# Two-block transformer kernel: fold order in block 1, last norm's weights on GpSimd, the last expert's slots in column halves

## The reference, cut to what matters

```python
# block 1
h = rmsnorm(x, norm1_g)
p = h @ w_in                                   # 1024 -> 1536: lru_x, lru_gate, four_in
c = centred_depthwise_conv(lru_x, conv_w, conv_b)
y_lru = gelu(lru_gate) * (rglru(c, ..., reverse=False) + rglru(c, ..., reverse=True))
y_four = real(fft2(four_in in 4 groups of 128, axes=(tokens, channels of the group)))
x = x + concat(y_lru, y_four) @ w_out
x = x + expert_choice_moe(rmsnorm(x, norm2_g)) # 16 experts, each takes its 64 best tokens
x = rmsnorm(x, normf_g)
# block 2: band attention, a diagonal state space model, gates
x = x + merged @ w_out_2
return rmsnorm(x, final_gain_2)
```

## Time and profile before

| what | value |
|---|---|
| median of 3 runs | 1468.22 us (1467.8 to 1468.32) |
| the profiled execution: its own time | 1466.85 us |
| the profiled execution: span, first to last instruction | 1465.0 us |
| mean granted TensorE clock | 0.998 of full speed |
| busy share: TensorE, VectorE, ScalarE, GpSimd | 94%, 37%, 23%, 8% |
| the chain that ended last: TensorE, transfers, VectorE, ScalarE | 62%, 30%, 4%, 2% |

### The profile page before, as it was taken

One profiled execution on the slowest core, in us unless ns is written; L12 is line 12 of the kernel. 1 busy time (PEld: TensorE's weight loads), 2 busy tenths in 40 slices (PEclk: granted clock), 3 DMA queues, 4 the chain that ended last, 5 costly groups with the idle time before them and its releaser, 6 DMA issues.

```text
span 1465.0 us, 16663 instructions
## 1 busy us (share of the span) xinstructions
PE 1373.4 (94%) x6713; PEld 737.6 (50%) x6713; DVE 547.6 (37%) x967; ACT 340.0 (23%) x549; POOL 114.5 (8%) x188
## 2 busy tenths in 40 slices
PE   7999999999998898998988988989999999999997
PEld 6778533333333232332322323323378787888876
DVE  7675621121211121121111211113278587756663
ACT  5893110010000010010000100103042465533322
POOL 0000000000000000000000000002022215550000
PEclk9999999999999999999999999999999999999999
DMA  9149899999999999999999999999975132353221
GB/s 324 22 168 390 329 421 405 429 428 429 429 429 429 429 429 429 429 429 429 429 429 429 429 427 429 429 428 428 420 242 132 58 105 83 83 173 133 94 107 58
DMA packets 67875, 467.05 MB, mean 319 GB/s; under 512 B 5744, under 2 KB 30576, under 8 KB 42608
## 3 DMA queue, kind: packets, MB, share of 16 engines
q1 hardware_dynamic: 63008, 454.71, 75.4%
q0 software_dynamic: 4528, 11.18, 3.1%
q10 hardware_dynamic: 288, 0.45, 0.1%
HBM read 458.22 MB, written 7.05 MB: 318 GB/s over the span
## 4 chain that ended last, share of the span: by engine, by line
PE 62%; DMA 30%; DVE 4%; ACT 2%; issue 2%; DVEq 0%; POOL 0%; ACTq 0%
DMA wide<-in_w_up 21%; PE bank L1035 13%; PE bank L975 12%; PE bank L727 8%; PE bank L728 8%; PE bank L729 8%; DMA early<-in_w_up 8%; PE bank L914 4%; PE bank L1005 1%; PE bank L1073 1%; DVE nrm L1749 1%; PE bank L1132 1%; PE bank L1160 1%; PE bank L757 1%; PE bank L762 0%
## 5 line engine op out<-in xcount | busy, mean ns | idle before, releaser
L975 PE MATMUL bank<-wide,xinT 128*64 128x512 f32 x1376 | 307.0, 596 | 41.9 <-DMA wide<-in_w_up 24.4
L975 PEld LDWEIGHTS bank<-wide,xinT 128*64 128x64 f32 x1376 | 96.6, 137 | 248.1 <-issue 170.8
L975 PE MATMUL bank<-early,xinT 128*64 128x512 f32 x656 | 147.0, 595 | 19.4 <-DMA early<-in_w_up 10.7
L1749 DVE SCALAR_TENSOR_TENSOR th<-th,bank 128x512 f32<-128x512 f32 x32 | 20.6, 684 | 385.2 <-ACT th L1458 385.2
L1035 PE MATMUL bank<-wide,actT 128*64 128x512 f32 x656 | 144.9, 594 | 3.6 <-issue 3.5
L727 PE MATMUL bank<-hT_lo,ring_r 128*128 128x512 f32 x352 | 138.6, 394 | 1.4 <-ACT gt L1323 1.1
L729 PE MATMUL bank<-hT_hi,ring_r 128*128 128x512 f32 x352 | 137.1, 390 | 0.0
L728 PE MATMUL bank<-hT_hi,ring_r 128*128 128x512 f32 x352 | 137.0, 389 | 0.0
L1458 ACT ACTIVATE th<-bank 128x512 f32<-128x512 f32 x32 | 17.4, 594 | 475.3 <-PE bank L975 475.3
L1746 DVE TENSOR_TENSOR ring_r<-ring,ring_r 128x2048 fp32r<-128x2048 f32 (+1 forms) x40 | 89.5, 2237 | 59.6 <-ACT ring_r L1291 59.2
L975 PEld LDWEIGHTS bank<-early,xinT 128*64 128x64 f32 x656 | 46.0, 137 | 118.5 <-issue 79.5
(11 more groups left out here) (427 smaller groups left out, 1705.7 us busy)
## 6 DMA issues: line engine op xcount, KB each, us to landing
wide<-in_w_gate SPq DMA_DIRECT2D x43, 2048.0 KB, 37.6
wide<-in_w_up SPq DMA_DIRECT2D x42, 2048.0 KB, 38.0
wide<-in_w_down SPq DMA_DIRECT2D x38, 2048.0 KB, 38.4
early<-in_w_down SPq DMA_DIRECT2D x21, 2048.0 KB, 38.5
early<-in_w_up SPq DMA_DIRECT2D x21, 2048.0 KB, 38.3
early<-in_w_gate SPq DMA_DIRECT2D x20, 2048.0 KB, 39.9
ring<-in_w_in SPq DMA_DIRECT2D x25, 1024.0 KB, 6.2
ring<-in_w_out SPq DMA_DIRECT2D x8, 1024.0 KB, 4.9
```

Of the source, the lines that this page charges most:

```text
L975: last = pe.matmul(bank[1 + 2 * (m % 2) + q // 2][o:o + 64, :], xinT[:, k, :], w[:, i, q * 512:(q + 1) * 512], start=(k == 0), stop=(k == ...
L1749: return dve.scalar_tensor_tensor(out_, a, s, b, op0, op1)
```

## The change

1. `folds()` becomes `even_folds()`, the sums, and `odd_folds()`, the clearing of column 0 and the differences. The scans of the second channel tile come between them. TensorE's `four` jobs are ordered by part first: both products of the sums wait for the first count of `folded`, both of the differences for the second.
2. `slot_hi` and `slot_lo` are made in two passes of 256 columns each; TensorE waits for each half by itself and runs the low products four steps behind the high ones.
3. GpSimd multiplies each merged half row by its weights `gfin` into `hT`, and VectorE's final pass multiplies that by the reciprocal alone. GpSimd's small addition of eps stands in its queue before the odd half row's product.

The diff:

```diff
@@ -353,6 +353,7 @@
         x_sums, gained, gained_sums = sem("x_sums"), sem("gained"), sem("gained_sums")
         x_root = sem("x_root")
         eps_set, deviation = sem("eps_set"), sem("deviation")
+        weighted = sem("weighted")
         gf_half_in, pairs_ready, slot_sums, slot_gained = (
             sem("gf_half_in"), sem("pairs_ready"), sem("slot_sums"), sem("slot_gained"))
         slot_root, slot_high, slot_low, slot_x2_ready, slot_x2_out = (
@@ -365,7 +366,7 @@
             jobs.add(f"xT{k}", k)
 
         order_b1 = [("in", 0), ("in", 1), ("in", 2), ("in", 3), ("lru", 0), ("in", 4), ("in", 5), ("lru", 1), ("in", 6),
-                    ("in", 7), ("lru", 2), ("in", 8)] + [("four", c) for c in range(2)] + [("mid", 0)] + [
+                    ("in", 7), ("lru", 2), ("in", 8)] + [("four", part) for part in range(2)] + [("mid", 0)] + [
             ("in", 9), ("in", 10), ("lru", 3)] + [("mix", g) for g in range(CT)] + [("in", 11)]
         W_LRU, W_DFT = 5, 6
         jobs.turn = 0
@@ -374,8 +375,8 @@
             if what == "in":
                 jobs.add(f"in{n}", unit=in_units[n // 2] if n % 2 else None)
             elif what == "four":
-                for half in range(2):
-                    jobs.add(f"four{n}_{half}")
+                for c in range(2):
+                    jobs.add(f"four{c}_{n}")
             elif what == "lru":
                 for i in range(4):
                     jobs.add(f"lru{n}_{i}", unit=W_LRU if (n, i) == (CT - 1, 3) else None)
@@ -826,15 +827,14 @@
                         split(unit)
                     project(f"in{n}", both(unit, 256), (n % 2) * P, (hT_hi, hT_lo), KT)
                 elif what == "four":
-                    if n == 0:
-                        pe.wait_ge(folded, 2)
-                    for part in range(2):
-                        b = start(f"four{n}_{part}")
-                        rows = (fold, mixT[:, CT:2 * CT, 0:HALF])[part]
+                    pe.wait_ge(folded, n + 1)
+                    rows = (fold, mixT[:, CT:2 * CT, 0:HALF])[n]
+                    for c in range(2):
+                        b = start(f"four{c}_{n}")
                         for g in range(CT):
-                            last = pe.matmul(b[:, g * P:(g + 1) * P], rows[:, g, n * P:(n + 1) * P],
-                                             dft[:, part * P:(part + 1) * P], start=True, stop=True)
-                        finish(f"four{n}_{part}", last)
+                            last = pe.matmul(b[:, g * P:(g + 1) * P], rows[:, g, c * P:(c + 1) * P],
+                                             dft[:, n * P:(n + 1) * P], start=True, stop=True)
+                        finish(f"four{c}_{n}", last)
                 elif what == "mid":
                     b = start("mid")
                     for g in range(CT):
@@ -1047,14 +1047,13 @@
                     other_rows(7)
                     other_rows(3, 4)
                     other_rows(6)
-                    lead = 5
-                    pe.wait_ge(slot_high, 1)
+                    lead = 4
                     for step in range(KT + lead):
-                        if step == lead:
-                            pe.wait_ge(slot_low, 1)
-                        for slots, at in ((slot_hi, step), (slot_lo, step - lead)):
+                        for slots, there, at in ((slot_hi, slot_high, step), (slot_lo, slot_low, step - lead)):
                             if 0 <= at < KT:
                                 k = Y_ORDER[at]
+                                if at % 4 == 0:
+                                    pe.wait_ge(there, at // 4 + 1)
                                 n, c = 64 * (k // 4), (k % 4) * P
                                 last = pe.matmul(bank[k][:, :], slots[n:n + 64, c:c + P], chosenT[n:n + 64, :],
                                                  start=False, stop=(slots is slot_lo))
@@ -1479,7 +1478,9 @@
             act_e.wait_ge(unit_used, last_of[B2_HI[0] // 2] + 1)
             act_e.activation(hi_of(M)[:, 0:UNIT // 2], ring[slot_of(M)][:, 0:UNIT // 2], ACT.Copy)
             act_e.wait_ge(slot_root, 1)
-            act_e.activation(slot_hi, th[:, 0, :], ACT.Copy, scale=stat[:, 50:51]).then_inc(slot_high, 1)
+            for h in range(2):
+                hs = slice(256 * h, 256 * h + 256)
+                act_e.activation(slot_hi[:, hs], th[:, 0, hs], ACT.Copy, scale=stat[:, 50:51]).then_inc(slot_high, 1)
             act_e.activation(hi_of(M)[:, UNIT // 2:UNIT], ring[slot_of(M)][:, UNIT // 2:UNIT], ACT.Copy).then_inc(w_hi, 1)
             scaled_hi("yT", "gb2", Y_ORDER)
             weights_hi(M + 1)
@@ -1727,10 +1728,15 @@
             pool.dma_start(yT, y_dram.rearrange("(c p) t j -> p c (t j)", p=P)).then_inc(y_in, 16)
             full(pool, f"pv{PAIRS - 1}")
             pool.dma_start(gfin, gfin_d.partition_broadcast(P)).then_inc(gfin_in, 16)
-            for t in range(TT):
-                c = stat[:, 48 + t:49 + t]
-                pool.wait_ge(square_sum, 2 * TT + 2 * t + 1)
-                pool.tensor_scalar(c, stat[:, 40 + 2 * t:41 + 2 * t], 1.0, EPS, ALU.mult, ALU.add).then_inc(half_sum, 1)
+            pool.wait_ge(gfin_in, 16)
+            for o in range(2 * TT):
+                t, h = o // 2, slice(o % 2 * 512, o % 2 * 512 + 512)
+                if o % 2:
+                    pool.wait_ge(square_sum, 2 * TT + o)
+                    pool.tensor_scalar(stat[:, 48 + t:49 + t], stat[:, 39 + o:40 + o], 1.0, EPS, ALU.mult,
+                                       ALU.add).then_inc(half_sum, 1)
+                was_read(pool, f"fin{o}")
+                pool.tensor_tensor(hT[:, o, :], added[:, t, h], gfin[:, h], ALU.mult).then_inc(weighted, 1)
 
         @block.vector
         def _(dve):
@@ -1828,13 +1834,17 @@
                     link(dve.tensor_tensor_scan(h, a, b, 0.0, ALU.mult, ALU.add))
                 tt(conv[:, c, :], gt[:, 0, 0, :], gt[:, 1, 0, :], ALU.add).then_inc(gt_free, 1)
 
-            def folds():
+            def even_folds():
                 for g in range(CT):
                     was_read(dve, f"in{CT + g}")
                 f = mixT[:, CT:2 * CT, :]
                 dve.tensor_copy(fold[:, :, 0:1], f[:, :, 0:1])
-                link(tt(fold[:, :, 1:HALF], f[:, :, 1:HALF], f[:, :, S - 1:HALF:-1], ALU.add))
-                dve.memset(f[:, :, 0:1], 0.0).then_inc(folded, 1)
+                tt(fold[:, :, 1:HALF], f[:, :, 1:HALF], f[:, :, S - 1:HALF:-1], ALU.add).then_inc(folded, 1)
+                dve.wait_ge(folded, 1)
+
+            def odd_folds():
+                f = mixT[:, CT:2 * CT, :]
+                link(dve.memset(f[:, :, 0:1], 0.0))
                 tt(f[:, :, 1:HALF], f[:, :, 1:HALF], f[:, :, S - 1:HALF:-1], ALU.subtract).then_inc(folded, 1)
 
             def unfold(g):
@@ -1869,8 +1879,9 @@
             recurrence_scans(0)
             weights_lo(4)
             recurrence_inputs(1)
-            folds()
+            even_folds()
             recurrence_scans(1)
+            odd_folds()
             weights_lo(W_DFT)
             weights_lo(7)
             recurrence_inputs(2)
@@ -2095,9 +2106,11 @@
             last_full(6, 2)
             link(dve.tensor_scalar(stat[:, 48:49], bank[6][:, 0:1], EPS, None, ALU.add))
             stt(stat[:, 49:50], stat[:, 48:49], EPS, bank[6][:, 1:2], ALU.mult, ALU.add).then_inc(bank_read[6], 1)
-            dve.wait_ge(slot_high, 1)
             dve.wait_ge(slot_gained, 1)
-            stt(slot_lo, th[:, 0, :], stat[:, 50:51], slot_hi, ALU.mult, ALU.subtract).then_inc(slot_low, 1)
+            for h in range(2):
+                hs = slice(256 * h, 256 * h + 256)
+                dve.wait_ge(slot_high, h + 1)
+                stt(slot_lo[:, hs], th[:, 0, hs], stat[:, 50:51], slot_hi[:, hs], ALU.mult, ALU.subtract).then_inc(slot_low, 1)
             dve.wait_ge(w_hi, split_units.index(M) + 1)
             halves_of = [tuple(v[:, i * UNIT // 2:(i + 1) * UNIT // 2] for v in (ring_r[slot_of(M)], ring[slot_of(M)], hi_of(M)))
                          for i in range(2)]
@@ -2405,9 +2418,9 @@
                     dve.wait_ge(deviation, TT + t + 1)
                     link(dve.reciprocal(stat[:, 52 + t:53 + t], stat[:, 52 + t:53 + t]))
                 for h in hs:
-                    r = added[:, t, 512 * h:512 * h + 512]
-                    stt(r, r, stat[:, 52 + t:53 + t], gfin[:, 512 * h:512 * h + 512], ALU.mult,
-                        ALU.mult).then_inc(final_ready, 1)
+                    dve.wait_ge(weighted, 2 * t + h + 1)
+                    dve.tensor_scalar(added[:, t, 512 * h:512 * h + 512], hT[:, 2 * t + h, :], stat[:, 52 + t:53 + t], None,
+                                      ALU.mult).then_inc(final_ready, 1)
 
             def merged_row(o):
                 r = added[:, o // 2, o % 2 * 512:o % 2 * 512 + 512]
```

## The result

| kernel | median | runs | profiled span |
|---|---|---|---|
| before | 1468.22 us (1465.81 to 1469.25) | 22 | 1465.0 us |
| after | 1470.32 us (1468.4 to 1472.08) | 22 | 1467.8 us |

The ratio is 1.0018, with a 95% interval of 1.0012 to 1.0024. The change costs 2.1 us. The interval does not hold 1, so the kernel after is slower, although by less than the 2.9 us that the prediction took for the least that could be told from no change. The forecast was 1467.8 and its range ended at 1469.8.

What follows compares the result with a forecast made beforehand. TensorE was taken to bound until about 400 us, the weight stream from 416 to 1043, then TensorE, with VectorE for the last 9 us. Terms -0.95 + 0.19 + 0.3 = -0.46 us gave 1467.8 us, range 1465.7 to 1469.8.

Steps and rivals of the forecast that it cites:

- The end is VectorE alone.: Last norm: VectorE's merges and final passes alone were taken to set the end, the last pass over at 1460.97 us.
- The last-norm part: Last norm, from 1447 us: weight products on GpSimd collide with VectorE's final passes; forecast loss 0.3 us.
- VectorE's walk: Last norm: pass-by-pass schedule with GpSimd collisions, last pass ending at 1461.25 against 1460.97 us, a loss of 0.3 us.
- product 7: Last norm: the last of GpSimd's eight weight products, numbered from 0, forecast to end at 1460.4 us.
- The third rival: Last norm: GpSimd's queue bounds the tail with products of 1.63 us; tail +2.1, sum +1.35, 1469.6 us; chance 0.07.
- thresholds of 1.53 and 1.90 us a product: Last norm: GpSimd product times from which the change turns slower (1.53) or slower by over 0.2% (1.90).
- the new stall for the differences: Folds: TensorE waits near 72.1 us for the differences, now made behind the scans; forecast 0.6 us.
- the bank free in time: Folds: the bank projection 9 writes is read at 75.23 us, nearly level with the differences, which end last.
- Does it carry through the stream?: Weight stream to 1043 us: the folds' 0.95 us was to shift it all; rival that it is lost: 1468.7, chance 0.10.
- The first rival: Last norm: VectorE passes and GpSimd products do not collide; tail -0.8, sum -1.56 us, 1466.7 us; chance 0.22.
- the rule: Last norm: a whole GpSimd product excludes a one-SBUF-source VectorE pass; five meetings at 0.25 us each, tail +1.5; chance 0.08.
- The rule's sum of +0.75: Whole change if GpSimd products and VectorE passes fully exclude each other: +0.75 us, 1469.0 us; chance 0.08.

Runs made afterwards that it cites:

- e2: The kernel before with only the last-norm edit (products with the weights on GpSimd): 1470.74 us, ratio 1.0023.
- e4: The kernel before with one GpSimd memset of one column added behind the last final pass: 1471.48 us, ratio 1.0024.
- e1: The kernel before with only the folds edit (scans between sums and differences, products ordered by part): 1467.06 us, ratio 0.9997.
- e6: The kernel before with the folds edit and the last row's addition of eps moved from GpSimd to VectorE: 1465.29 us, ratio 0.9982.
- e3: The kernel before with the last row's addition of eps moved from GpSimd to VectorE, behind the last merge: 1466.05 us, ratio 0.9986.

## Why the prediction was wrong

**The step that failed: "The end is VectorE alone."** The last-norm part walks VectorE's passes to 1461.25 and stops there, as the chain of waits did. What ended the kernel before was GpSimd's drain, 7.2 us behind its last instruction. The term that is missing is GpSimd's own: its last instruction moves from 10.08 to 13.17 us behind the first merge, +3.1 us, all of it exposed (that is, it lengthens the run by as much), because the drain ended last already. With +3.1 in place of the +0.3 of VectorE's walk, the prediction's own sum is -0.95 + 0.19 + 3.1 = +2.3 us, and the median gave +2.1. e2 shows it with that edit alone, +2.8. The needed number was in the prediction: product 7 "to 1460.4", against 1457.61 for the last operation before. These 2.8 us in place of the 0.3 would have given a sum of +2.0 and a time of 1470.3. And the profile before showed the exposure in the gap from 1460.97, VectorE's last pass, to the span's end at 1465.0, which I read as the stores. The walk said "The stores of the output follow each pass on SyncE and move with the last", without asking which of the engines closes the program. The third rival, GpSimd's queue as the bound, had the right engine and the right sign; but it let the end hang on VectorE's last pass behind GpSimd's products, and gave 1469.6. It needed products of 1.63 us for that; they took 1.33, so its nearness to 1470.32 is luck. (Its thresholds of 1.53 and 1.90 us a product hold the 0.08 to the next one; for the product alone the same sum gives 1.46 and 1.82.)

**Edit 1** was forecast at 0.95 and measured 0.89 at projection 9 and 0.87 at the first load. The steps are as written: scans 1.13 us earlier against the sums, the new stall for the differences (0.33 us by the row, which counts from the end of the pair's tail, 0.5 from the pair's 1.78; 0.6 forecast), the bank free in time. The second pair took 1.98 us instead of 1.8.

**Does it carry through the stream?** The profiled executions can't tell. From the first load to the start of the last expert's closing products they take from 961.6 (e2) to 964.1 us (e4), 962.2 before and 963.3 in the kernel after, without order by edit. In the kernel after about a microsecond of the head start went between 208 and 248 us, where the transfers moved 392 GB/s against 403 in the matching stretch before (40 us x 11/403 = 1.1 us, an estimate); the wait of the earlier trace rows then ended no earlier against block 1's first product than before (440.7 us behind it against 440.4). The medians are for it: -0.9 in e1, and e6 stands 2.7 below before where e3 stands 1.9 below. The kernel after against e2, with the 0.2 of edit 2 set aside, gives -0.9 again. Each comparison alone has an interval that holds 0. All 181 times on record, fitted together by least squares (an estimate, with one term for each edit and one level for each of the three sets of runs), give edit 1 a gain of 0.7 us, with a 95% interval of 0.3 to 1.1. So some of the head start reaches the end, if the edits add up as the fit takes it; that all 0.87 do is not shown.

**Edit 2** was forecast at +0.19 and measured 0.2 on the path, by the mechanism named: ScalarE's copy starts 0.82 behind the first pass. TensorE's wait in front of block 2 grew from 0.55 to 1.12, since its slot products now end earlier and it waits for the same split.

**Edit 3, VectorE's share**, was forecast at +0.3 and measured +0.41. The first rival (no collision) is wrong. The passes paid most: each pass that met a product ended about 0.3 us behind that product's end. The products paid little: GpSimd's eight took 1.30 to 1.48 us, their median 1.33, and only the three that began while a pass was running took 1.38 or more. My walk had let a product near a pass take up to 1.6. The Trainium skill, "SBUF — State Buffer", section "Who interferes with whom", has the two exclude each other for the whole instruction. This trace agrees with an exclusion nearly that strict: of a pass's 0.48 us about 0.2 lay under the product. But the price that I put on the rule, +1.5 us for the tail, was too high: the tail on VectorE lost 0.41, near the +0.3 of the forecast. The rule's sum of +0.75 lies nearer to the measured +2.1 by luck, for it too leaves out the term that decided.

## What to carry to other kernels

Before costing an edit near the end of a program, read the closing instructions of every engine and not only the chain of waits, and ask which engine lets the program end. In this kernel it was the later of two: GpSimd's last instruction plus 7.2 us, and SyncE's last store. Work that is put on GpSimd late pays by when it ends, whatever it takes off VectorE; even one column of 128 x 1, moved to VectorE, was worth 1.9 us of 1468 (e3), and with the folds 2.7 us (e6, ratio 0.9982, below both kernels).

## What the runs showed of the hardware

- GpSimd's closing drain ends 7.2 us behind its last instruction in all nine kernels, be that a memset of 0.10 us, an addition of 0.19 us or a product of 1.38 us. VectorE's ends 0.05 us behind its last pass (1461.02 for a last pass over at 1460.97). What GpSimd does in these 7.2 us no view shows.
- A one-scalar pass of VectorE (128 x 512, SBUF to SBUF) takes 0.48 us alone, 0.49 when it meets only the last 0.2 to 0.3 us of a GpSimd product, and 0.70 to 1.19 when it starts earlier under one; it ends 0.28 to 0.32 us behind the product's end. A product that begins while such a pass runs takes 1.38 to 1.52 us, the others 1.30 to 1.34. VectorE's merges, which read PSUM, keep their 0.69 us beside the same products.
- Block 1's first product starts between 14.07 and 15.27 us in nine profiled executions, and the stream's length spreads by 2.5 us: a single profile can't show an edit of 1 us by its span, but it shows it by differences taken near the edit, to 0.04 us.
